# Where additions and normalisations stand in VectorE's queue, and down banks among up banks: FFN and differential attention on one Trainium2 core

## What is computed

```python
def diff_attend(q, k, v, lam_params, lam_init, subln_w):
    ...
        p1 = softmax(einsum("bhqd,bhkd->bhqk", q1, k1) * scale)
        p2 = softmax(einsum("bhqd,bhkd->bhqk", q2, k2) * scale)
        return einsum("bhqk,bhkd->bhqd", p1 - lam * p2, v)
    ...
    o = rms_norm(o, subln_w) * (1.0 - lam_init)

def conv_ffn(h, w_up, conv_w, conv_b, w_down):
    u = h @ w_up
    up = pad(u, ((0, 0), (1, 1), (0, 0)))
    u = up[:, :s] * conv_w[0] + up[:, 1:s + 1] * conv_w[1] + up[:, 2:s + 2] * conv_w[2] + conv_b
    g, val = split(u, 2, axis=-1)
    return (silu(g) * val) @ w_down
```

## Time and profile before

| | |
|---|---|
| median of 3 runs | 4038.33 us (4037.52 to 4045.91) |
| the profiled execution | 4043.29 us, span on the core 4041.6 us |
| mean granted clock of TensorE | 0.931 |
| TensorE busy | 3478.5 us (86%), 20703 matmuls |
| VectorE, ScalarE, GpSimd busy | 1832.4, 1173.4, 937.5 us (45, 29, 23%) |
| differential attention | about 250 to 1075 us |
| FFN of layer 0, of layer 1 | about 1180 to 2070 us, 3120 to 4014 us |

### The profile page before, as it was taken

The page is one execution under the profiler, slowest core; times in us unless marked ns, Lnnn a source line. Parts: engine busy times, 40 slices in busy tenths (PEclk is TensorE's granted clock), DMA queues, the critical chain, the costliest instruction groups (busy, mean ns, idle before and its releaser), DMA issues. The chain is left out here.

```text
span 4041.6 us, 53521 instructions
## 1 busy us (share of the span) xinstructions
PE 3478.5 (86%) x20703; PEld 3181.1 (79%) x20703; DVE 1832.4 (45%) x2407; ACT 1173.4 (29%) x2115; POOL 937.5 (23%) x733
## 2 busy tenths in 40 slices
PE   5388898888799999999955788888779999999997
PEld 1178888887689999999955667666669899999996
DVE  0434545455245555455451244444333645554554
ACT  0234444444232211111131244444342322111211
POOL 0212222222233222222231122222114222212221
PEclk7699989998899999999977899999999999999998
DMA  9421111112211110111022322222241111101101
GB/s 391 205 67 41 41 41 41 41 36 103 76 42 42 53 42 31 36 52 36 21 69 66 81 65 67 65 75 77 81 153 56 42 32 52 42 31 36 52 26 52
DMA packets 209506, 268.94 MB, mean 67 GB/s; under 512 B 31396, under 2 KB 174365, under 8 KB 202077
## 3 DMA queue, kind: packets, MB, share of 16 engines
q1 hardware_dynamic: 201373, 244.23, 19.3%
q0 software_dynamic: 7856, 22.29, 1.6%
q10 hardware_dynamic: 144, 0.52, 0.0%
HBM read 198.57 MB, written 35.91 MB: 58 GB/s over the span
## 5 line engine op out<-in xcount | busy, mean ns | idle before, releaser
L454 PE MATMUL psum<-Hh,wh 128*128 128x384 f32 x3264 | 1122.7, 344 | 111.5 <-POOL wl L1438 38.2
L455 PE MATMUL psum<-Hh,wl 128*128 128x384 f32 x3264 | 1110.7, 340 | 0.0
L456 PE MATMUL psum<-Hl,wh 128*128 128x384 f32 x3264 | 1108.7, 340 | 0.0
L454 PEld LDWEIGHTS psum<-Hh,wh 128*128 128x128 f32 x3264 | 629.1, 193 | 124.7 <-POOL wl L1438 38.5
L455 PEld LDWEIGHTS psum<-Hh,wl 128*128 128x128 f32 x3264 | 629.1, 193 | 0.0
L456 PEld LDWEIGHTS psum<-Hl,wh 128*128 128x128 f32 x3264 | 627.9, 192 | 0.0
L535 DVE SCALAR_TENSOR_TENSOR x<-psum,mod,x 128x384 f32<-128x384 f32 (+2 forms) x768 | 375.2, 514 | 470.0 <-PE psum L456 425.6
L454 PE MATMUL psum<-ff_ah,ff_dh 128*128 128x384 f32 x1056 | 375.4, 356 | 70.0 <-DVE x L535 47.4
L948 DVE SCALAR_TENSOR_TENSOR ff_c<-ff_u,par,ff_c 128x1153 f32<-128x1153 f32 x176 | 374.2, 2126 | 15.6 <-DVE ff_c L945 2.8
L945 DVE TENSOR_SCALAR ff_c<-ff_u,par 128x1153 f32<-128x1153 f32 x88 | 124.1, 1411 | 532.4 <-ACT ff_u L777 532.4
L817 POOL TENSOR_TENSOR wl<-wr,wh 128x1024 fp32r<-128x1024 f32 x88 | 222.5, 2529 | 611.0 <-ACT wh L744 611.0
(11 more groups left out here) (218 smaller groups left out, 4715.8 us busy)
## 6 DMA issues: line engine op xcount, KB each, us to landing
in_mw<-mod_w SPq DMA_DIRECT2D x48, 1024.0 KB, 8.8
wr<-w_up SPq DMA_DIRECT2D x88, 512.0 KB, 3.9
ff_dr<-w_down SPq DMA_DIRECT2D x22, 1024.0 KB, 6.0
wr<-w_qkv_diff SPq DMA_DIRECT2D x24, 512.0 KB, 3.9
ga_ks<-k_save SPq DMA_DIRECT2D x8, 1280.0 KB, 5.5
x<-x_save SPq DMA_DIRECT2D x16, 576.0 KB, 8.8
ga_qsh<-ga_nqh SPq DMA_DIRECT2D x32, 288.0 KB, 4.8
ga_qsl<-ga_nql SPq DMA_DIRECT2D x32, 288.0 KB, 5.4
```

Source lines behind the costliest of these rows:

```text
L454: pe.matmul(out, w_hi, m_hi, start=start, stop=False)
L455: pe.matmul(out, w_lo, m_hi, start=False, stop=False)
L456: return pe.matmul(out, w_hi, m_lo, start=False, stop=stop)
```

## The change

In the FFN the 24 down banks of group i - 1 go out in six parts of four. A part follows each of the three banks of unit 1 and each of the three banks of unit 2 of group i. VectorE's order follows: two convolution steps of unit 0; additions 0 to 3; the third step; additions 4 to 11; two steps of unit 1; additions 12 to 15; the third; additions 16 to 19; the product; additions 20 to 23. The splits of the first product and of the down weights move from unit 1 to unit 2, on ScalarE and GpSimd. In the first group, which has no down banks, VectorE's order stays. The down product of the last group is issued as before.

In the differential attention `normalise` is called in front of `maxima` in a step and at the end of a head.

```diff
@@ scalar, FFN
                     if j % 2:
-                        q = 2 * i + j // 2
                         act.wait_ge(b.conv, 3 * (4 * i + j))
                         act.activation(b.c[:, j - 1, :], b.c[:, j - 1, :], ACT.Silu).then_inc(b.silu, 1)
-                        act.wait_ge(b.prod, q + 1)
-                        if j == 1 and not first:
+                    if j >= 2:
+                        k = j - 2
+                        act.wait_ge(b.prod, 2 * i + k + 1)
+                        if k == 0 and not first:
                             act.wait_ge(b.dn_mm, DN * i)
...
-                    if j == 1:
+                    if j == 2:
                         act.wait_ge(b.d_in, 16 * (i + 1))
                         act.activation(b.dh[:, :, :], b.dr[:, :, :], ACT.Copy).then_inc(b.d_hi, 1)
@@ gpsimd, FFN
-                    if j % 2:
-                        pool.wait_ge(b.a_hi, 2 * i + j // 2 + 1)
...
+                    if j >= 2:
+                        k = j - 2
+                        pool.wait_ge(b.a_hi, 2 * i + k + 1)
...
-                    if j == 1:
+                    if j == 2:
                         pool.wait_ge(b.d_hi, i + 1)
@@ tensor, FFN
                 for n in range(NN):
                     last = linear_bank(g, pe, 3 * (j % 2) + n, g.wh[:, j % 2], g.wl[:, j % 2], n)
-                last.then_inc(b.up_mm, 1)
+                    if n == NN - 1:
+                        last.then_inc(b.up_mm, 1)
+                    if j in (1, 2) and not first:
+                        down_part(i - 1, 12 * (j - 1) + 4 * n, fresh=isinstance(i, int) and i == 1)
...
+            def down_part(i, first_x, fresh=False, count=4):
+
+                if first_x == 0:
+                    pe.wait_ge(b.a_lo, 2 * i + 2)
+                    pe.wait_ge(b.d_lo, i + 1)
+                    if fresh:
+                        pe.wait_ge(b.xr_d, KC * NN)
+                for x in range(first_x, first_x + count):
+                    if not (fresh and x < 2):
+                        pe.wait_ge(b.dn_add, DN * i + x - 1)
+                    down_bank(x, x // NN, x % NN)
...
-                    down(i - 1, fresh=isinstance(i, int) and i == 1)
@@ vector, FFN
-                for s in range(3):
-                    conv(i, 0, s)
-                if first:
-                    for s in range(3):
-                        conv(i, 1, s)
-                    mult(i, 1)
-                else:
-                    for x in range(DN):
+                conv(i, 0, 0)
+                conv(i, 0, 1)
+                for x in range(DN):
+                    if not first:
                         add_bank(i - 1, x, isinstance(i, int) and i == 1)
-                        if x in (1, 3, 5):
-                            conv(i, 1, (x - 1) // 2)
-                        if x == 7:
-                            mult(i, 1)
+                    if x == 3:
+                        conv(i, 0, 2)
+                    if x == 11:
+                        conv(i, 1, 0)
+                        conv(i, 1, 1)
+                    if x == 15:
+                        conv(i, 1, 2)
+                    if x == 19:
+                        mult(i, 1)
@@ vector, differential attention
                 for s in range(TILES):
+                    for p in BC_AT.get(s - 1, []):
+                        normalise(ring, h, p)
                     if s:
                         maxima(h, s)
-                    for p in BC_AT.get(s - 1, []):
-                        normalise(ring, h, p)
...
                 for p in ST_AT[TILES]:
                     mean_square(ring, p)
+                for p in BC_AT[TILES]:
+                    normalise(ring, h, p)
                 if ahead:
                     maxima(after(h, 1), 0)
-                for p in BC_AT[TILES]:
-                    normalise(ring, h, p)
```

More of the change, by code:

```diff
@@ L780, in body @@
                     if j % 2:
-                        q = 2 * i + j // 2
                         act.wait_ge(b.conv, 3 * (4 * i + j))
                         act.activation(b.c[:, j - 1, :], b.c[:, j - 1, :], ACT.Silu).then_inc(b.silu, 1)
-                        act.wait_ge(b.prod, q + 1)
-                        if j == 1 and not first:
+                    if j >= 2:
+                        k = j - 2
+                        act.wait_ge(b.prod, 2 * i + k + 1)
+                        if k == 0 and not first:
                             act.wait_ge(b.dn_mm, DN * i)
-                        act.activation(b.ah[:, j // 2, 0:NS], b.c[:, j, 0:NS], ACT.Copy)
-                        act.activation(b.ah[:, j // 2, NS:T], b.c[:, j, NS + 1:PADT], ACT.Copy).then_inc(b.a_hi, 1)
-                    if j == 1:
+                        act.activation(b.ah[:, k, 0:NS], b.c[:, 2 * k + 1, 0:NS], ACT.Copy)
+                        act.activation(b.ah[:, k, NS:T], b.c[:, 2 * k + 1, NS + 1:PADT], ACT.Copy).then_inc(b.a_hi, 1)
+                    if j == 2:
                         act.wait_ge(b.d_in, 16 * (i + 1))
@@ L834, in body @@
                         w_lo(i + (j + 2) // 4, (j + 2) % 4)
-                    if j % 2:
-                        pool.wait_ge(b.a_hi, 2 * i + j // 2 + 1)
[L837 to L840, removed]
-                    if j == 1:
+                    if j >= 2:
+                        k = j - 2
+                        pool.wait_ge(b.a_hi, 2 * i + k + 1)
+                        pool.tensor_tensor(b.al[:, k, 0:NS], b.c[:, 2 * k + 1, 0:NS], b.ah[:, k, 0:NS].bitcast(F32), ALU.subtract)
+                        pool.tensor_tensor(b.al[:, k, NS:T], b.c[:, 2 * k + 1, NS + 1:PADT],
+                                           b.ah[:, k, NS:T].bitcast(F32), ALU.subtract).then_inc(b.a_lo, 1)
+                    if j == 2:
                         pool.wait_ge(b.d_hi, i + 1)
@@ L918, in _ @@
             if not nx:
-                down(GROUPS - 1, fresh=False)
+                down_part(GROUPS - 1, 0, count=DN)
                 return
```

## The result

The changed kernel takes 3944.9 us (median of 4 runs, 3943.1 to 3948.6) where the kernel before takes 4037.9: a ratio of 0.9766, 95% interval 0.9749 to 0.9783. The forecast was 3940 us. Between the two profiled executions the span falls from 4041.6 to 3946.8 us, by 94.8.

What follows compares the result with a forecast made beforehand. TensorE was taken as the bound, so only its idle and low-clock time could be won: FFN 66 + attention 32 = 98 us off 4043.3, and 5.0 less for the median, gives 3940 us; range 3915 to 3988.

Steps and rivals of the forecast that it cites:

- FFN, 66 us: FFN loop: each body loses 1.0 us in place of 4.3, so 3.3 us x 20 = 66 us are won.
- The body of 75.8 us: FFN sign: a body of 75.8 us with one idle, 0.5 to 1 us, before the third down bank.
- B: FFN: both pairs of convolution steps meet GpSimd's work, so 4.3 us a body stay lost; 4006 us, chance 0.08.
- D: FFN: `al` of the second product becomes the bound, 100 us lost, 4106 us in all; chance 0.04.
- the step of 2.75 us: FFN, earlier trace: a convolution step between additions, 1.41 us alone, 2.75 us where GpSimd works on SBUF.
- Steps 5 and 7, 27 and 15 us: Attention: normalisation before maxima gains 3.8 us at step 5 and 2.1 at step 7, in seven heads each.
- The undisturbed step that I took as a model: Attention: a step with a projection, 8.6 us, including a transposition of keys; step 5 was forecast at 8.3.
- what is late next: Attention, step 7: the rotation of the queries is late next, leaving TensorE idle about 1.6 us before step 8's transposes.
- 0.3 of the 1.2 us: Step 7: if its new idle lowers the clock, 1.2 us of the 2.4 us gain are lost; 2.1 was taken.
- End of a head, -15 us: Attention: maxima wait for spreads and last normalisation; 1.7 us plus 0.4 for low clock, 15 us lost in seven heads.
- rival A: Attention pays most back: low clock after step 7's idle, 3.1 us at a head's end; 3954 us, chance 0.14.
- idles of 1.9 us leave the clock at 0.99: FFN before the change: idles of 1.9 us with granted clock 0.99, taken to disagree with the skill's rule on clock swings.

Runs made afterwards that it cites:

- kernel 7: Changed kernel with one convolution step of unit 0 in front of the down banks in place of two; 3935.7 us, ratio 0.9729 to before.
- kernel 4: Changed kernel with the 24 down banks in one piece behind unit 1, VectorE's new order kept; 4004.1 us, ratio 0.9924 to before.
- kernel 8: Changed kernel with all three convolution steps of unit 0 in front of the additions; 3994.3 us, ratio 0.9872 to before.
- Kernel 9: Changed kernel with GpSimd's split of the down weights one unit later; 4018.2 us, ratio 0.9930 to before.
- kernel 3: Changed kernel with the next head's maxima again in front of the last two normalisations at a head's end; 3926.2 us, ratio 0.9723 to before.
- kernel 2: Only the attention part of the change, with the FFN of the kernel before; 4003.0 us, ratio 0.9912 to before.
- kernel 6: Changed kernel with a fourth piece of the rotation of the queries put into step 7; 3958.7 us, ratio 0.9797 to before.

## Why the prediction was right, point by point

**FFN, 66 us: right, 63 measured (31 and 32).** The order of events was as worked out: the second step held beside `wl` (3.42 us, I had 3.59), the third addition late, a stall there and no other. The body of 75.8 us measured 75.9, but two errors cancel in it. Of the stall, 0.9 us forecast, 0.5 came (0.35 of it as idle). The rest of the body was taken as 74.8 us, from 0.173 us a matmul, and 0.1 of small ones; kernel 7, in which TensorE never waits, shows that it takes 75.3. The 3 us by which the FFN fell short are most of the 5 us between the forecast and the median. The term that was a little too large is the gain per body, 3.3 us forecast against 79.1 - 75.9 = 3.2, 64 us in 20 bodies. Kernels 4, 7 and 8 bear out the mechanism: what counts is how much VectorE work stands between an up bank and the third down bank behind it. Rivals B and D did not happen. Kernel 9 shows a delay of the kind that D feared, with `dl` in place of `al`: one unit later, it costs 3.1 us a body. One reading was wrong without harm: the step of 2.75 us in the earlier trace rows is a first step (L945), which takes 0.88 us alone, not 1.41; the sum does not use it.

**Steps 5 and 7, 27 and 15 us: both a little small.** Step 5 fell from about 12.3 us on average to 7.98 (4.35 us, my upper bound was 4.1), 30 us in seven heads. The undisturbed step that I took as a model had a transposition of keys in it, and I gave that 0.3 us of its own; step 5 came out 0.6 below the model. Step 7 fell by 2.7 on average, 19 us. The forecast of what is late next was exact: an idle of 1.66 us before the transposes of step 8, ended by `da_e`. Whether that idle lowers the clock was the open point, and the runs show no simple answer. Seven kernels have this idle in each of seven heads; it was followed by the lower clock in one head of the changed kernel, in three of kernel 3, in two of kernel 7, in six of kernels 2 and 4, and in all seven of kernels 8 and 9. The attention of kernels 2, 4, 7, 8 and 9 is that of the changed kernel, instruction for instruction. Kernel 2's heads take 98.0 to 99.0 us all the same: in four of its six the fall stands in step 8 in place of near the end of the head, and the time at 1.2 GHz in such a head is the same 10.2 us; in the other two it is 6.8. I had put only 0.3 of the 1.2 us into the sum, and the total bears that out, the reason less so.

**End of a head, -15 us: too small, -17 to -21 measured.** The order cost 1.8 us, as forecast (1.7): the last score is out at 652.7 and the maxima start at 654.49. The undersized term is the clock, 0.4 us a head; kernel 3 has 22.2 us less time at 1.2 GHz in seven heads, which is worth about 1.6 us a head. In the changed kernel the stretch behind it is the slowest of a head:

```profile
650.00:664.00 14.00, 9.90 (x48) 9.04 (x45) 5.35 (x8) 3.83 (x7) 7.59 (x14) 0.64 0.19 63
```

and kernel 3 in its stretch:

```profile
638.00:652.00 14.00, 11.45 (x61) 10.30 (x62) 5.66 (x10) 4.38 (x9) 7.04 (x12) 0.76 0.17 54
```

I had read in the trace of before that the transposes of values could start 1.5 us sooner and that it would buy nothing. True, but with the spreads done earlier TensorE has less to do in that wait: its idle before transposes of values is 4.1 us a head (25.1 + 3.6 over seven) against 2.6 in kernel 3 (12.6 + 5.6), and there is more time at 1.2 GHz around it. Of rival A (3.1 us at the end of a head) this half nearly came true, and its other half, step 7, did not. The errors of steps 5, 7 and the end cancel: 32 us forecast for the attention, 32 measured. That the two agree so closely is luck.

**The clock.** The prediction argued that in the FFN idles of 1.9 us leave the clock at 0.99 and that this speaks against the Trainium skill's page "TensorE: Matmul & The Clock Gate", section "A second HAM failure mode: psum-queue depth-cycling". Kernel 8 corrects that: the same 1.92 us, once per body, was followed by the lower clock in 12 of 18 bodies. By that section's rule this is to be expected. A mean of 0.99 over nine bodies had hidden it: in the kernel before, too, 3 of 9 bodies in each layer took 79.8 to 80.2 us in place of 78.65, and they are the ones with a fall. The measurement and the page agree on the direction, and I was wrong to count the mean as a contradiction. It did not harm the sum, because the lower clock of before was inside the 79.1 us.

**What stays open.** Why a given idle is followed by the lower clock in one body and not in the next one, with the same matmuls around it, is not settled by these runs; only its frequency is measured. The length of the idle alone does not decide it, as the counts in the last section show.

## What to carry to other kernels

Where two engines meet through two small buffers, put the side work of the second behind a long piece of the first that doesn't need the buffers, and count how much side work stands in front of the *third* hand-over: 0.9 us of it was hidden completely, 4.3 left 0.35 us of idle, 5.9 left 1.9. After moving an operation forward at the top of a loop, look at each other place where the same move is made; here one edit in three was a loss of 17 to 21 us, hidden under the two that won. And where a stall goes, read the next thing in the queue of the engine that caused it: one instruction of 1.2 us in each head, moved out of the way of the new idle, was worth 24 us.

## What the runs showed of the hardware

- How often an idle of TensorE was followed by the lower clock (it began during the idle or at most 2 us behind it):

| idle, us | where | followed by 1.2 GHz |
|---|---|---|
| 0.35 | FFN, changed kernel | 0 of 20 |
| 1.5 to 1.6 | FFN, kernel 4 | 0 of 20 |
| 1.66 | step 8, changed kernel, 2, 3, 4, 7, 8, 9 | 32 of 49 |
| 1.9 | FFN, before | 6 of 20 |
| 1.9 | FFN, kernel 2 | 4 of 20 |
| 1.7 to 1.9 | FFN, kernel 8 | 12 of 20 |
| 2.1 to 2.2 | FFN, kernel 9 | 3 of 20 |
| 2.5 | step 8, kernel 6 | 6 of 7 |
| 2.6 to 2.7 | steps 5 and 7, before | 16 of 16 |

  A fall cost about 1.6 us in the FFN, in matmuls at 0.32 us in place of 0.17. In kernel 8 an idle of 1.9 us thus costs its own length and, in the mean, 12 x 1.6 / 20 = 1.0 us more.
- A convolution step of VectorE and a split of GpSimd that overlap in time lengthen each other, and either can be the loser. In kernel 9 a step of 0.88 us took 3.98 beside a split of 4.60, which kept its length. In kernel 4 GpSimd lost as well: its subtraction, 2.00 us elsewhere, took 3.53 where a step had begun before it.

```profile
1511.73 3.43 DVE L950 SCALAR_TENSOR_TENSOR ff_c<-ff_u,par,ff_c 128x1153 f32<-128x1153 f32 x1 [0.15 <-DVE ff_c L947]
...
1513.89 3.53 POOL L839 TENSOR_TENSOR ff_al<-ff_c,ff_ah 128x1024 fp32r<-128x1024 f32 x1
```

  The Trainium skill, page "SBUF — State Buffer", section "Who interferes with whom", says that whichever issues first holds the shared ports for its whole instruction; these rows agree. The prediction told that section's rule, that an instruction with at most one SBUF input does not contend, without its exception: the page excepts VectorE's two-port modes. The first step, a TENSOR_SCALAR with one tensor as its input, was held in kernel 9 (3.98 us) and in the earlier trace rows (2.75 us). An addition, which has one input in PSUM, was not held: in the changed kernel 54 additions lie inside a `wl`, and none took more than 0.62 us.
